# A two-layer diffusion trunk on one core: copies, mixing matmuls and one modulation chunk change places

## The reference, cut to what matters

```python
for l in range(DEPTH):                      # DEPTH = 2
    mod = sc @ w_mod[l] + b_mod[l]          # 12 chunks of 512 columns: shifts, scales, gates
    h = modulate(x, norm1_g[l], sh1, s1)
    y, yc = token_mixers(h, hc, l, not last, p)   # 4 mixers, each gated by a sigmoid, then w_out
    x = x + g1 * y
    h2 = modulate(x, norm2_g[l], sh2, s2)
    x = x + g2 * hier_moe(h2, ...)          # 16 experts, 2 per token

u = jax.nn.silu(xblk @ w1[e]) * (xblk @ w3[e])    # gate matrix w1, up matrix w3
return u @ w2[e]                                  # down matrix w2
```

## Time and profile before

| | |
|---|---|
| median of 3 runs | 1535.5 us (1534.55 to 1535.86) |
| the profiled execution's own time | 1536.32 us |
| its span (first to last instruction) | 1534.3 us |
| PE busy | 1444.5 us (94%) |
| DVE busy | 765.5 us (50%) |
| ACT busy | 277.5 us (18%) |
| POOL busy | 165.4 us (11%) |
| DMA | 355.55 MB, mean 232 GB/s |
| experts of layer 0 | about 640 to 917 us |
| experts of layer 1 | 1306 to 1526 us |

### The profile page before, as it was taken

One profiled execution on the slowest core, in us unless ns is written; L12 is line 12 of the kernel. 1 busy time (PEld: TensorE's weight loads), 2 busy tenths in 40 slices (PEclk: granted clock), 3 DMA queues, 4 the chain that ended last, 5 costly groups with the idle time before them and its releaser, 6 DMA issues.

```text
span 1534.3 us, 17006 instructions
## 1 busy us (share of the span) xinstructions
PE 1444.5 (94%) x6200; PEld 718.8 (47%) x6200; DVE 765.5 (50%) x1689; ACT 277.5 (18%) x570; POOL 165.4 (11%) x156
## 2 busy tenths in 40 slices
PE   6999999999999999999999999999988899999887
PEld 2544644444544445522222225765866765333322
DVE  4297867586766978422122125686585525111112
ACT  3201101333321202210110102111243202000000
POOL 0000011011212100111112001001011210110100
PEclk9999999999999999999999999999999999999999
DMA  9520234202224355699999967317324596999995
GB/s 378 199 90 28 75 145 164 83 28 82 83 87 165 119 211 220 253 380 423 408 404 415 412 263 275 136 56 274 113 80 149 207 351 233 385 413 416 423 419 224
DMA packets 49536, 355.55 MB, mean 232 GB/s; under 512 B 6288, under 2 KB 6672, under 8 KB 22704
## 3 DMA queue, kind: packets, MB, share of 16 engines
q1 hardware_dynamic: 41360, 330.79, 54.9%
q0 software_dynamic: 4800, 14.24, 2.6%
q10 hardware_dynamic: 3296, 9.44, 1.6%
HBM read 343.88 MB, written 10.56 MB: 231 GB/s over the span
## 4 chain that ended last, share of the span: by engine, by line
PE 77%; DVE 12%; DMA 4%; issue 3%; SPq 3%; ACT 1%; DVEq 0%; POOL 0%; ACTq 0%; POOLq 0%
PE ps L1206 23%; PE ps L1512 19%; PE ps L1219 6%; PE ps L1522 6%; PE ps L1390 6%; PE ps L1307 4%; SPq L981 2%; DVE n_ L2386 2%; DMA hT<-w 2%; PE ps L1534 1%; PE ps L1180 1%; DMA ring<-wmod 1%; DVE mx L2517 1%; PE ps L1343 1%; PE ps L1291 1%
## 5 line engine op out<-in xcount | busy, mean ns | idle before, releaser
L1206 PE MATMUL ps<-hT,ring 128*128 128x512 f32 (+1 forms) x1344 | 448.2, 488 | 1.9 <-DVE hT L2337 1.3
L1206 PEld LDWEIGHTS ps<-hT,ring 128*128 128x128 f32 x1344 | 251.6, 190 | 181.2 <-issue 158.0
L1512 PE MATMUL ps<-ring,m 128*64 128x512 f32 x624 | 278.5, 598 | 20.3 <-ACT m L1961 10.0
L1512 PEld LDWEIGHTS ps<-ring,m 128*64 128x64 f32 x624 | 82.4, 137 | 201.0 <-issue 183.8
L2299 DVE SCALAR_TENSOR_TENSOR spare<-ring,crow 128x1024 bf16<-128x1024 f32 x120 | 166.2, 1385 | 4.1
L1219 PE MATMUL ps<-ring,hT 128*128 128x512 f32 (+1 forms) x352 | 125.1, 515 | 0.0
L2024 POOL TENSOR_TENSOR wide<-wide,gates 128x512 f32<-128x512 f32 (+1 forms) x48 | 69.1, 1441 | 376.9 <-DVE gates L2476 376.8
L1514 PE MATMUL ps<-n_,m 128*64 128x512 f32 x224 | 101.7, 603 | 0.0
L1307 PE MATMUL ps<-yT,ring 128*128 128x512 f32 (+1 forms) x256 | 94.8, 493 | 1.3 <-ACT yT L1883 1.3
L1514 PE MATMUL ps<-wide,m 128*64 128x512 f32 x208 | 93.7, 597 | 0.0
L1219 PEld LDWEIGHTS ps<-ring,hT 128*128 128x128 f32 x352 | 66.7, 190 | 55.1 <-issue 51.4
(11 more groups left out here) (389 smaller groups left out, 1693.4 us busy)
## 6 DMA issues: line engine op xcount, KB each, us to landing
ring<-w SPq DMA_DIRECT2D x39, 2048.0 KB, 11.1
ring<-win SPq DMA_DIRECT2D x52, 1024.0 KB, 4.9
ring<-wmod SPq DMA_DIRECT2D x48, 1024.0 KB, 5.1
n_<-w SPq DMA_DIRECT2D x13, 2048.0 KB
hT<-w SPq DMA_DIRECT2D x13, 2048.0 KB, 16.6
wide<-w SPq DMA_DIRECT2D x13, 2048.0 KB
ring<-wbr SPq DMA_DIRECT2D x8, 1024.0 KB, 4.9
ring<-wout SPq DMA_DIRECT2D x4, 2048.0 KB, 8.9
```

Source lines behind the costliest of these rows:

```text
L1206: last = pe.matmul(b[:, 0:W], w[:, k, jj * P:(jj + 1) * P], hT[:, k, 0:W], start=(k == 0), stop=(k == KD - 1))
L1512: pe.matmul(ps[0:HALF, bnk, :], left[:, k, 0:HALF], even[k], start=(k == 0), stop=(k == n_k - 1), skip_group_check=True)
```

## The change

The code changes in three places.

**ACT in the experts of layer 0.** The copy of one half of the side up result becomes a function of its own, called behind `turned_u`.

**PE in the experts of layer 1.** `mix(e - 1)` runs whole, between gate(e) and up(e); `turn_u(e)` follows up(e) directly, and down(e) follows `turn_u(e)`.

**The modulation of layer 1.** Chunk 9 leaves the second attention for the last gates, and the last gates' modulation steps are spread over two thirds of them instead of one half.

```diff
-        with_za, with_conformer, in_c, behind, with_wo = [(1, 6), (1, 7)], [], [(1, 8), (1, 9)], [(1, 10), (1, 11)], []
+        with_za, with_conformer, in_c, behind, with_wo = [(1, 6), (1, 7)], [], [(1, 8)], [(1, 9), (1, 10), (1, 11)], []
...
-    n = len(last_gates) if l == 0 else len(last_gates) // 2
+    n = len(last_gates) if l == 0 else len(last_gates) * 2 // 3
...
-                    def mix_block(first, last_, signal=True, tiles=range(live(l))):
-                        for t in tiles:
+                    def mix_block(first, last_, signal=True):
+                        for t in range(live(l)):
...
-                    def mix(e, turn=None):
+                    def mix(e):
...
-                        mix_block(e == 0, e == PAIRS - 1, True, range(0, 1))
-                        if turn is not None:
-                            turn_u(turn)
-                        mix_block(e == 0, e == PAIRS - 1, True, range(1, 2)).then_inc(y_mixed, 1)
+                        mix_block(e == 0, e == PAIRS - 1).then_inc(y_mixed, 1)
...
                             four_quarters(7, side_xT, split_k(wg, wg2)).then_inc(side_gate_done, 1)
+                        if not side and e:
+                            mix(e - 1)
                         weights_landed("w3", e)
...
                         gate_and_up(e)
-                        if not side and e:
-                            mix(e - 1, e)
-                        elif not side:
+                        if not side:
                             turn_u(e)
...
                         act.activation(side_act, side_gate, ACT.Tanh, scale=0.5).then_inc(side_tanh, 1)
+
+                    def side_up_part_of(e):
                         act.wait_ge(side_up_done, e + 1)
                         act.activation(side_up_part, ps[HALF:P, 6, :], ACT.Copy).then_inc(side_up_copied, 1)
...
                         turned_u(e)
+                        if side:
+                            side_up_part_of(e)
                         result(e)
```

## The result

The changed kernel takes 1527.19 us in the median (1523.99 to 1527.99, 6 runs), the kernel before 1535.68 us (1532.64 to 1537.34, 6 runs) beside it: a ratio of 0.9942 (95% interval 0.9928 to 0.9956), which is faster by 8.9 us (the ratio is estimated from all runs; the medians alone lie 8.5 us apart). The forecast was 1526.5 us. Measured once more, in a later series (5 runs, 9 of the kernel before), the ratio is 0.9910 (0.9894 to 0.9926), 13.8 us. The two intervals do not touch, so the size of the gain is known to some 2.5 us only; their mean is 11.4 us. The profiled executions lie 11.1 us apart (1536.32 and 1525.23 us, spans 1534.3 and 1523.1).

What follows compares the result with a forecast made beforehand. PE plus 1.29 us of ACT bounds layer 0's experts, a DVE and ACT chain the second attention, the weight stream layer 1's experts. Terms -8.4 + 0.3 - 0.9 = -9.0 us give a 1526.5 us median; range 1522.5 to 1531.5.

Steps and rivals of the forecast that it cites:

- The copy in layer 0: Layer 0's experts: swapping ACT's two copies takes 1.29 us a pair off PE's chain; 8.4 us faster, between 7.8 and 10.3.
- the prediction's own sign: Forecast is wrong if the span from 640 to 917 shrinks by less than 7 or more than 10.3 us.
- The mis-sized term: Layer 0's experts: DMA was taken to be the limit, since 427 GB/s would be needed and neither experts stage holds it.
- the 2 us of late waits: Layer 0's later pairs: PE waits on weight loads, summing to about 2 us; none would be rival 1.
- Rival 1: DMA has headroom in layer 0 and the output weights are in time: -11.9 us, 1523.6 us; chance 0.17.
- the ceiling of 10.3: Layer 0's experts: the most the copy swap could gain, 8 pairs x 1.29 us off PE's chain.
- The modulation chunk: Layer 1: attention ends 4.2 us earlier, but late output weights cost the projection 4.5 us; +0.3 us in sum.
- the forecast's bound of +1.8: Layer 1's output projection: starts 1.8 us later than before if the 8.4 MB queued take the full 25.6 us.
- The mixing products: Layer 1's experts: mixing fills the last pair's wait and the gap behind up shrinks; -0.9 us, bounds -1.9 to 0.
- rival 4: Layer 1's experts: late ends of up release buffers late, the stream runs dry; +4.1 us, 1539.6 us; chance 0.06.
- rival 3: Layer 1's weight stream ends at its old time, giving back the front's gain; -0.9 us left, 1534.6 us; chance 0.08.
- The sum: Whole kernel: -8.4 + 0.3 - 0.9 = -9.0 us, giving 1527.3 us for the profiled execution and 1526.5 for the median.

Runs made afterwards that it cites:

- the output weights first: Changed kernel with 4.2 MB of expert weights issued behind the two output weights instead of ahead of them: 1516.96 us, ratio 0.9871; again 1519.08 us, 0.9885.

## Why the prediction was right

**The copy in layer 0** was forecast at -8.4 us and measured at -11.3. The mechanism held: both copies off the chain, down at the end of side up, nothing new late. But by the prediction's own sign the size was wrong, since the stage shrank by more than 10.3 us. The mis-sized term is DMA's. I took 415 GB/s for a limit, about the highest rate of the windows before (417). With the limit at 424 the deficit is 0.63 us a pair instead of about 1, the weights in hand cover it, and none of the 2 us of late waits that I expected appear. Rival 1 (nothing lost to DMA) was the better account of this stage, though at 424 GB/s and not at the 435 it leaned on. Its other half, output weights in time, did not come. A further 0.11 us a pair came from products that no longer start behind a stop; the ceiling of 10.3 had left it out.

**The modulation chunk** was forecast at -4.2 us in the attention and +4.5 at the projection. The attention gave 4.55; the third pair of units gave 1.2 where 0.8 were expected. The projection starts with a wait of 4.45 us, 3.7 more than its old gap. With the 0.6 us lost ahead of the attention and 0.2 among the gates the stage comes to 0.0 against the +0.3. The landing was forecast well, 24.1 us behind the issue of chunk 11's second half, and measured 23.4, but the way there is another: the forecast queued the output load right behind the 4.2 MB, while in fact it was held 6.2 us for its place in the ring and then landed in 13.04. What the step lacked is the clock behind the wait, +2.7 us in the trace. With it the edit costs 1.9 us in this trace, at the forecast's bound of +1.8; alone it measures +2.0 in the runs (0.3 to 3.7) and +0.7 in its trace.

**The mixing products** were forecast at -0.9 and measured at -1.0 in the trace and -0.8 alone (not told from none). The gap of 2.2 us between up and down came out, and the stream did not starve (415 GB/s at a share of 1.01), so rival 4 is out. So is rival 3: the first expert of layer 1 starts 10.4 us earlier, the last pair's gate weights land 10.2 us earlier. An earlier end of the mixers moved the whole stream.

**The sum** of -9.0 was right by two errors of opposite sign: 2.9 us more from layer 0, 2.7 us less from the projection. The 11.2 us of the spans contain 1.85 us of clock at the end of layer 0 that is no part of the change, and the mean of the two measurements says that the true size may be nearer 11 than 9. The time of 1526.5 was met more closely than its terms deserve; that part was luck.

## What to carry to other kernels

A DMA share of 1.00 is no sign of the limit (it went with 406 to 425 GB/s here); how much the stream can still give was seen when PE was made to wait for it, by leaving matmuls out. Before work is moved between two stages, look at what the receiving stage's loads queue behind: here about 4 us of gain were lost to one late load and came back by issuing it ahead of 4.2 MB that nobody needed yet. When a wait is gone, look whether the load came earlier or its reader later. Price a wait of several microseconds on PE with the slower products behind it.

## What the runs showed of the hardware

- The granted clock falls to 0.50 behind a wait of 4.45 us on PE, and products run at the lower of its two levels (1.2 GHz) for some 5 us: +2.7 us over 64 products. Behind waits of 4.36 us (the modulation edit alone) it was +1.6, and 4.98 us (the second trace of the changed kernel) +2.8. Behind a wait of 0.86 us, with fillers ahead, it stays at 1.00.
- Such a drop comes or stays away from one execution to the next at places with the same work: 3.62, 4.20 and 5.08 us for the same 32 transposes at the end of layer 0; 3.86 and 5.49 us for 32 products L1190; and behind the attention's wait of 2.04 us, 3.62 us for sixteen gate products in the kernel before and 5.30 with ACT's swap alone. Two traces of one kernel, the output weights first, differ by 2.3 us between layer 1's first gate product and the projection (292.2 and 294.5).
- One core alone draws 424 GB/s from weights, gathers and stores together when DMA sets the pace (layer 0), and 415 in layer 1, where homes in several pieces are loaded; why that stage has less was not tried.
- The same kernel's ratio differed by 0.0032 between two series, more than the intervals of either measurement allow.
